# Projection stage of a hybrid encoder layer: weight splits moved to VectorE, the RG-LRU recurrence spread channel by channel, a turned beta/decay product at the start

## What is computed

```python
proj = x @ w_in                       # 1024 -> 6 * 1024 channels, and 16 more for beta and decay
qkv_raw, z, b_raw, a_raw, lx, ly = split(proj)
qkv = silu(causal_dwconv(qkv_raw))    # depthwise, 4 taps
beta = sigmoid(b_raw)
g = -exp(a_log) * softplus(a_raw + dt_bias)
...                                   # gated delta rule over q, k, v, beta, g; gated by silu(z)
xc = causal_dwconv(lx) + b            # RG-LRU branch
r = sigmoid(xc @ wa + ba)             # block diagonal, 8 blocks of 128
i = sigmoid(xc @ wx + bx)
log_a = 8 * r * log_sigmoid(lambda)
a = exp(log_a)
mult = sqrt(1 - exp(2 * log_a))       # 1 at position 0
h[t] = a[t] * h[t-1] + mult[t] * i[t] * xc[t]
lru_out = h * gelu(ly)
```

## Time and profile before

| what | us |
|---|---|
| median of 3 runs | 1669.2 (1666.99 to 1671.74) |
| the profiled execution, time | 1664.48 |
| the profiled execution, span | 1662.7 |
| TensorE busy | 1513.0 |
| VectorE busy | 1027.1 |
| ScalarE busy | 598.2 |
| GpSimd busy | 468.4 |
| projection stage, from the start to the last tile's reading | 364.9 |

### The profile page before, as it was taken

One profiled execution on the slowest core, in us unless ns is written; L12 is line 12 of the kernel. 1 busy time (PEld: TensorE's weight loads), 2 busy tenths in 40 slices (PEclk: granted clock), 3 DMA queues, 4 the chain that ended last, 5 costly groups with the idle time before them and its releaser, 6 DMA issues. The chain is left out here.

```text
span 1662.7 us, 21050 instructions
## 1 busy us (share of the span) xinstructions
PE 1513.0 (91%) x8028; PEld 1140.9 (69%) x8028; DVE 1027.1 (62%) x1633; ACT 598.2 (36%) x860; POOL 468.4 (28%) x297
## 2 busy tenths in 40 slices
PE   7999689989899997699998899999999999999664
PEld 7999689988898886344433666777776677767321
DVE  4815998605566575135452777777777777766376
ACT  3346323332303302000001555555555555555201
POOL 2423554422133231003212233332222111232023
PEclk9999789998989997799999899999999999999885
DMA  5222112210000000630034799999999999998393
GB/s 199 77 77 64 51 63 84 82 52 1 1 1 1 1 1 14 248 141 14 26 131 181 289 362 374 376 367 372 372 372 362 365 364 362 362 366 336 115 410 101
DMA packets 53158, 313.21 MB, mean 188 GB/s; under 512 B 14928, under 2 KB 15952, under 8 KB 34320
## 3 DMA queue, kind: packets, MB, share of 16 engines
q1 hardware_dynamic: 33312, 276.16, 43.6%
q0 software_dynamic: 19760, 35.89, 5.8%
HBM read 301.33 MB, written 42.12 MB: 207 GB/s over the span
## 5 line engine op out<-in xcount | busy, mean ns | idle before, releaser
L1856 DVE TENSOR_TENSOR gate_up_lo<-wide,gate_up_hi 128x2048 fp32r<-128x2048 f32 x128 | 293.0, 2290 | 96.1 <-ACT gate_up_hi L1799 94.6
L325 PE MATMUL bank<-x_hi,w_hi 128*128 128x274 f32 x768 | 231.0, 301 | 32.1 <-POOL w_lo L287 23.3
L1799 ACT ACTIVATE gate_up_hi<-wide 128x2048 fp32r<-128x2048 f32 x128 | 244.5, 1913 | 7.4 <-PEq L1195 7.4
L327 PE MATMUL bank<-x_hi,w_lo 128*128 128x274 f32 x768 | 227.8, 297 | 0.0
L326 PE MATMUL bank<-x_lo,w_hi 128*128 128x274 f32 x768 | 227.4, 296 | 0.0
L1727 PE MATMUL bank<-gate_up_hi,rows_hi 128*128 128x512 f32 x512 | 206.4, 403 | 8.0 <-DVE rows_lo L1865 8.0
L1729 PE MATMUL bank<-gate_up_hi,rows_lo 128*128 128x512 f32 x512 | 200.9, 392 | 0.0
L1728 PE MATMUL bank<-gate_up_lo,rows_hi 128*128 128x512 f32 x512 | 200.2, 391 | 0.0
L1665 POOL DMA_INDIRECT expert_rows<-lru,slot_ids x64 | 98.2, 1535 | 332.5 <-DVE lru L1872 317.7
L325 PEld LDWEIGHTS bank<-x_hi,w_hi 128*128 128x128 f32 x768 | 150.4, 196 | 34.5 <-POOL w_lo L287 29.7
L287 POOL TENSOR_TENSOR w_lo<-w_raw,w_hi 128x1024 fp32r<-128x1024 f32 x48 | 119.1, 2483 | 186.9 <-ACT w_hi L388 186.9
(11 more groups left out here) (276 smaller groups left out, 2437.3 us busy)
## 6 DMA issues: line engine op xcount, KB each, us to landing
wide<-in_w_exp SPq DMA_DIRECT2D x64, 2048.0 KB
wide<-in_w_exp SPq DMA_DIRECT2D x43, 1024.0 KB
w_raw<-in_w_in SPq DMA_DIRECT2D x48, 512.0 KB, 3.3
last_down<-in_w_exp SPq DMA_DIRECT2D x21, 1024.0 KB
expert_rows<-expert_rows SPq DMA_DIRECT2D x8, 2048.0 KB, 12.8
wide<-in_w_out SPq DMA_DIRECT2D x1, 3584.0 KB, 22.1
wide<-in_w_out SPq DMA_DIRECT2D x1, 2560.0 KB, 14.0
zt<-in_x_t SPq DMA_DIRECT2D x2, 1096.0 KB, 7.0
```

The costliest lines, as they stand in the source:

```text
L325: nc.tensor.matmul(out, wh[:, k, :], x_hi[:, k, at], start=(k == 0), stop=False)
L327: last = nc.tensor.matmul(out, wl[:, k, :], x_hi[:, k, at], start=False, stop=(k == DC - 1))
L1799: nc.scalar.activation(half(w_hi[b % 2], u), half(w_gu[b % RAW], u), ACT.Copy).then_inc(s_whi, 1)
L1856: nc.vector.tensor_tensor(half(w_lo[b % 2], u), half(w_gu[b % RAW], u), half(w_hi[b % 2], u), ALU.subtract).then_inc(s_wlo, 1)
```

## The change

The weight splits L287 go from GpSimd to VectorE. In tiles that are convolved the split of the tile two ahead stands behind the first convolution step, in the others it comes first. GpSimd keeps only its memsets. The recurrence is done for one channel block at a time: gate products come after tiles 3 to 10 instead of 8 to 15, Square from tile 5 on, the squared multiplier from tile 8, Sqrt at tiles 11 to 13, scans at tiles 12 to 15, two each, with the memset, scaling and the output product on VectorE too. `ly` is read with a plain copy; gelu follows at tiles 15 and 16. The 16 beta/decay channels are computed first of all, with the weights stationary and the tokens moving (8 slices, 2 halves of 274 columns); VectorE copies them to SBUF and TensorE turns them with five small products by an identity, in the middle of tile 0. `w_ba` is loaded ahead of x. The decay sums come after tile 2. Loops on ScalarE, VectorE and GpSimd are written out; TensorE's loop over tiles 16 to 47 stays.

```diff
             load(0, 0, True)
+            sp.dma_start(w_ba, dram["w_ba"]).then_inc(s_wba, 16)
             for half in range(2):
                 ks = slice(4 * half, 4 * half + 4)
                 sp.dma_start(x_t[:, ks, :], dram["x_t"][:, ks, :]).then_inc(s_x[half], 16)
             load(1, 1, True)
-            sp.dma_start(w_ba, dram["w_ba"]).then_inc(s_wba, 16)
...
-            with pool.Fori(0, 11) as pair:
-                for i in range(2):
-                    split(pair * 2 + i, i)
-            scale_input(0)
-            scale_input(1)
-            for j in range(8):
-                if j % 2 == 0:
-                    split(22 + j // 2, (j // 2) % 2)
-                if j < 6:
-                    scale_input(j + 2)
-                pool.wait_ge(s_lru, j + 1)
-                pool.tensor_tensor(lru[:, j, :], lru[:, j, :], mult[:, j, :], ALU.mult).then_inc(s_lru_out, 1)
...
+                if isinstance(n, int) and n == 0 and half == 0:
+                    turn_ba(pe)
...
+        def project_ba(pe):
+
+            pe.wait_ge(s_wba, 16)
+            for k in range(DC):
+                if k % 4 == 0:
+                    pe.wait_ge(s_x[k // 4], 16)
+                for half in range(2):
+                    last = nc.tensor.matmul(mem.bank[4 + half][0:2 * H, 0:HALF], w_ba[:, k, :],
+                                            x_t[:, k, half * HALF:(half + 1) * HALF],
+                                            start=(k == 0), stop=(k == DC - 1))
+            last.then_inc(s_ba_t, 1)
+
+        def turn_ba(pe):
+
+            pe.wait_ge(s_const, 32)
+            pe.wait_ge(s_ba_copied, 1)
+            for t in range(TILES + 1):
+                at, w = (t * P, P) if t < TILES else (S0, DEC)
+                last = nc.tensor.matmul(mem.bank[6][0:w, 16 * t:16 * t + 16], ba_t[:, at:at + w],
+                                        C("ident")[0:2 * H, 0:2 * H], start=True, stop=True)
+            last.then_inc(s_ba, 1)
...
+            project_ba(pe)
             for n in range(16):
                 project(pe, n, n % 8, n < 2)
...
+                if 3 <= n <= 10:
+                    project_gates(pe, n - 3)
...
+            for n in range(8):
+                evacuate(n)
+                split(n + 2)
...
+                if n >= 3:
+                    gate(n - 3)
+                if n >= 5:
+                    square(n - 5)
+            for n in range(8, 16):
+                act.wait_ge(s_proj, n + 1)
+                two_halves(n, halves(lru[:, n - 8, :]), ACT.Copy).then_inc(s_psum, 1)
+                split(n + 2)
+                if n <= 10:
+                    gate(n - 3)
+                for b in {8: (3, 4), 9: (5,), 10: (6,), 11: (7,)}.get(n, ()):
+                    square(b)
+                for b in {11: (0, 1, 2, 3), 12: (4, 5), 13: (6, 7)}.get(n, ()):
+                    root(b)
+                if n == 15:
+                    for b in range(4):
+                        gelu(b)
+            for n in range(16, 40):
+                evacuate(n)
+                split(n + 2)
+                if n == 16:
+                    for b in range(4, 8):
+                        gelu(b)
+                else:
+                    silu(n - 9)
+            silu(31)
...
+            def split(m):
+
+                if m < NCH:
+                    dve.wait_ge(s_whi, m + 1)
+                    nc.vector.tensor_tensor(w_lo[m % 2], w_raw[m % 2], w_hi[m % 2], ALU.subtract).then_inc(s_wlo, 1)
+
+            def convolve(n):
...
+                steps.done(nc.vector.tensor_scalar(acc, r[:, 0:TW], weight[:, m, 0:1], PR("conv_b")[:, m:m + 1],
+                                                   ALU.mult, ALU.add))
+                split(n + 2)
+                for k in range(1, CONV):
+                    steps.wait()
...
+            def scan(b):
+
+                dve.wait_ge(s_mult, b + 1)
+                steps.link(nc.vector.memset(mult[:, b, 0:1], 0.5))
+                steps.link(nc.vector.tensor_tensor(t_i[:, b, :], t_i[:, b, :], mult[:, b, :], ALU.mult))
...
+            for n in range(8):
+                convolve(n)
+                if n >= 4:
+                    gated(n - 4)
+            for n in range(8, 16):
+                split(n + 2)
+                if n < 12:
+                    gated(n - 4)
+                for b in {8: (0, 1), 9: (2, 3), 10: (4, 5), 11: (6,), 12: (7,)}.get(n, ()):
+                    squared_multiplier(b)
+                if n >= 12:
+                    scan(2 * n - 24)
+                    scan(2 * n - 23)
+            for n in range(16, 40):
+                convolve(n)
...
+                for b in {23: (6, 7)}.get(n, (n - 17,) if 17 <= n < 23 else ()):
+                    lru_output(b)
+            for n in range(40, NCH):
+                split(n + 2)
```

More of the change, by code:

```diff
@@ new lines, in turn_ba, with project_gates @@
+        def turn_ba(pe):
[6 more added lines that the diff above has]
+            last.then_inc(s_ba, 1)
+        def project_gates(pe, b):
+            if b == 0:
+                pe.wait_ge(s_gates, 16)
+                pe.wait_ge(s_gread, 1)
+            pe.wait_ge(s_conv, b + 1)
+            if b:
+                pe.wait_ge(s_gateread, b)
+            for m in range(2):
+                for half in range(2):
+                    last = nc.tensor.matmul(mem.bank[4 + 2 * m + half][:, 0:HALF], gates[:, m * DC + b, :],
+                                            xc[:, b, half * HALF:(half + 1) * HALF], start=True, stop=True)
+            last.then_inc(s_gate, 1)
@@ L330, in _ @@
         @block.tensor
         def _(pe):
+            project_ba(pe)
             for n in range(16):
                 project(pe, n, n % 8, n < 2)
-                if n == 0:
-                    pe.wait_ge(s_wba, 16)
-                    for t in range(TILES + 1):
-                        at, w = (t * P, P) if t < TILES else (S0, DEC)
-                        for k in range(DC):
-                            last = nc.tensor.matmul(mem.bank[4][0:w, 16 * t:16 * t + 16], x_t[:, k, at:at + w],
-                                                    w_ba[:, k, :], start=(k == 0), stop=(k == DC - 1))
-                    last.then_inc(s_ba, 1)
@@ new lines, in evacuate, with gate @@
+            def evacuate(n):
+                act.wait_ge(s_proj, n + 1)
+                m = n if n < 8 else n - 8
+                if m >= 4:
+                    act.wait_ge(s_conv, m - 3)
+                two_halves(n, halves(raw[m % 4][:, GAP:RW]), ACT.Copy).then_inc(s_psum, 1)
+            def gate(b):
+                act.wait_ge(s_gate, b + 1)
+                for m, out in enumerate((t_r, t_i)):
+                    for half, part in enumerate(halves(out[:, b, :])):
+                        last = nc.scalar.activation(part, mem.bank[4 + 2 * m + half][:, 0:HALF], ACT.Tanh,
+                                                    bias=gate_half[:, m * DC + b:m * DC + b + 1], scale=0.5)
+                last.then_inc(s_gateread, 1)
+                act.wait_ge(s_gateread, b + 1)
+                nc.scalar.activation(mult[:, b, :], t_r[:, b, :], ACT.Tanh, bias=c_neg[:, b:b + 1],
+                                     scale=c_neg[:, b:b + 1])
+                nc.scalar.activation(t_r[:, b, :], t_r[:, b, :], ACT.Exp, bias=c_lru[:, b:b + 1],
+                                     scale=c_lru[:, b:b + 1]).then_inc(s_a, 1)
@@ L391, in _, with silu @@
+            def silu(m):
+                act.wait_ge(s_conv, m + 1)
+                nc.scalar.activation(qkv[:, m - 8, :], conv[m % 2], ACT.Silu).then_inc(s_fin, 1)
+            split(0)
             for k in range(DC):
@@ L456, in _ @@
[L456 to L462 removed]
+                    act.wait_ge(s_softp, 1)
+                if n >= 3:
[3 more added lines that the diff above has]
+            for n in range(8, 16):
+                act.wait_ge(s_proj, n + 1)
+                two_halves(n, halves(lru[:, n - 8, :]), ACT.Copy).then_inc(s_psum, 1)
[9 more added lines that the diff above has]
+                        gelu(b)
```

211 lines of the change are left out of this document (67 added, 144 removed).

## The result

| | before | after |
|---|---|---|
| median of the runs beside each other | 1668.1 us (1661.84 to 1671.74, 4 runs) | 1626.05 us (1624.05 to 1626.47, 4 runs) |
| profiled execution / its span | 1664.48 / 1662.7 | 1625.87 / 1624.0 |
| tile 1 read by ScalarE | 33.88 | 32.78 |
| tile 15 read | 132.91 | 133.66 |
| tile 47 read (last `zt` read) | 364.86 | 329.07 |

The ratio is 0.9758, 95% interval 0.9738 to 0.9777. The changed kernel is 42 us faster by the medians and 38.7 by the two spans (38.7 forecast; 1630.5 forecast for the median, 1626.05 measured). At the last read of a tile, where the changed stage ends, it is 35.8 us ahead.

A forecast was written before the change was run, and what follows sets the result against it. TensorE, busy 91%, was taken as the bound, losing time where `w_lo` came late. Winning 34.6 + 4.1 = 38.7 us gives 1625.8 profiled; 4.7 more for the median gives 1630.5, range 1623 to 1643.

The forecast's parts named there:

- The loss behind tile 15: Projection, after tile 15: 34.6 us lost, 23.3 in waits for `w_lo`, 11.3 mostly half-speed matmuls; all forecast to come back.
- the all-channel operations: Recurrence: single operations over all channels hold back each engine's own tiles; forecast to disappear with the per-channel form.
- the pause from 165.1 to 177.03: GpSimd makes no split then: it waits 9.33 us for the memset behind the all-channel square root, then scales two channels.
- Stretching by GpSimd: VectorE beside GpSimd splits: a three-element instruction takes 2.36 us instead of 0.17, scalar-tensor-tensor steps 1.151 in the mean instead of 0.79.
- The rival that needed it to stay without GpSimd (1683): VectorE becomes the bound: stretching stays, 8.3 us per tile, 52.7 lost against 38.7 won, 1683 us; chance 0.04.
- The start: Before tile 1 is read: turned beta/decay product first, read at 29.8 against 33.88, 4.1 us won.
- the slow phase: First matmuls at the start run slowly for 3.3 us, forecast to cost 1.7 us.
- `w_ba`'s delay: Start: 64 KB of `w_ba` ahead of x on SP's queue delay x by 0 to 2.3 us; 0.5 taken.
- The low-clock rival: Start: turned product stays at the low clock, takes 13.2 us, tile 1 read at 36.2; 32.3 won, 1636.9 us; chance 0.17.
- The sum: Whole kernel: 34.6 + 4.1 = 38.7 us won, giving 1625.8 for the profiled execution and 1630.5 for the median.
- Order stalls: Tiles 11 to 17 each slip 2 us as splits queue on VectorE; 14 of 34.6 stay lost, 1644.5 us; chance 0.13.
- The change does what it says: Opposing rival: the 170 to 230 gap remains from serial recurrence work, 34.6 not won, 1665 us; chance 0.03.

## Why the prediction was right

**The loss behind tile 15 comes back whole: right, 34.6 forecast, 34.7 measured.** So were its steps: no wait for `w_lo` from tile 2 on, STTs at 0.788, splits at 1.223, the beat at 6.11, the granted clock 1.00 from 20 on, GpSimd without tensor work in the stage (0.56 us, its memsets).

**The reason I gave for it was only part of it.** I began with GpSimd's queue: splits behind memset, scalings and scans. The runs say: splits off GpSimd, 10.3 of 34.6; products off GpSimd, 8.6; GpSimd's order, 0.1; the recurrence rearranged, with the splits left on GpSimd, all of it. So the rearranged recurrence is the cause, per channel and begun at tile 3, with much of it in tiles 8 to 15, where VectorE has no convolution and was busy for 9.78 of 60 us. That its place matters is shown by the late scans (7.8 us back); the larger part is something else in the rearrangement. Two candidates stand in the traces and were not run alone: the all-channel operations, which the prediction named (some 5.1 us of ScalarE for the Sqrt ahead of tile 20's reading), and ScalarE's wait for all eight scans ahead of tile 24, which it did not name. How the 34.6 divide stays open. Its reading of the pause from 165.1 to 177.03 was wrong as well: `w_hi` for the next split was begun only at 174.67, so the wait for the memset and the two scalings behind it cost that split 1.2 us.

**Stretching by GpSimd: right as a mechanism, without a price of its own.** It is real (0.788 to 1.060, and 10.8 us of the stage when VectorE also has the splits) and hidden where VectorE has room. The rival that needed it to stay without GpSimd (1683) did not come.

**The start is the term that was mis-sized: 4.1 us forecast, 1.1 measured against the earlier trace rows.** Two steps of it: x was put 0.5 later and was 1.9 later (1.4); the product was put at 6.6 + 1.7 and took 9.9 (1.6). Of these 1.6, 1.0 is the price of its rows, which I took from the gate products: behind tile 0 it takes 7.58, not 6.6. The other 0.6 is the slow phase, 2.3 and not 1.7. I had put `w_ba`'s delay near its lower bound because of its size; the middle of the bounds (0 and 2.3) was nearer. The low-clock rival did not come: 13.2 would have been the time of a wholly slow product. Against the slower executions of the old product the start wins 4.7, so the forecast's 4.1 is not excluded as a mean; it is not shown either.

**The sum hides that error, by luck.** 38.7 forecast, 38.7 between the spans: 34.7 + 1.1 + 2.9, the last from stages whose code is unchanged. From the last `zt` read to the end it took 1297.8 us before and 1294.9 after, but 1297.3 in the second profile of the same changed kernel, and 1288.5 to 1300.6 over all fourteen profiles. The 2.9 us are inside that spread. The stage alone gave 35.8. The median stands 42 below the one beside it, and 4.4 below the forecast, because I added the 4.7 between the profiled execution and the median of the runs; the changed kernel's profiled execution lies 0.2 from its median.

**The rivals.** Order stalls: no TensorE wait in tiles 11 to 17; but the split made twice shows that the slack was thinner than the 3 us I gave it. The change does what it says.

## What to carry to other kernels

When one engine is named as late, follow what it waits for itself, gate by gate, before blaming its queue: the wait was for GpSimd's `w_lo`, and with GpSimd's order mended TensorE only came sooner to ScalarE's wait for the scans. Count the work of the engines that feed it, tile by tile, against the beat; here VectorE had idle time 60 us earlier. A serial side computation belongs in the tiles where its engine is idle, in pieces that fit under a beat; then even a slower and stretched engine can make the splits at no cost. And before crediting a start-up edit, look at the same stretch in several profiles, since its clock is not the same in each.

## What the hardware showed that I had not expected

- A 64 KB load between two larger ones on the same queue held the next back by 1.9 to 2.9 us (x at 8.95 to 9.89 in six profiles, against 7.02), ahead of both by 0.5 (7.51).
- The same 80 matmuls of 16 columns, TensorE busy throughout and behind a tile at a granted clock of 1.00, took 9.58 us in one profile and 11.93 in another, with granted clocks of 0.66 and 0.50 from 20 to 30; 0.50 is the lower of the two levels, 1.2 GHz, for the whole stretch. The Trainium skill's "TensorE: Matmul & The Clock Gate", Part 1, says a busy array is released to 2.4 GHz; for this narrow product none of the five profiles that have it agrees (0.66 in three, 0.50 in two).
- The granted clock stands at 1.00 in the stretches of the start too, though the turned product took 9.92 us there against 7.58 behind tile 0. The column can't price the start; the lengths of the matmuls can. The changed kernel's stretch:

```profile
10.00:20.00 10.00, 10.00 (x39) 4.28 (x38) 6.90 (x11) 4.52 (x8) 0.00 (x0) 1.00 0.79 301
```

- Stages with unchanged code, summed, took 1288.5 to 1300.6 us over fourteen profiles; a gain of a few microseconds can only be read at the stage's own end.
